# Start places of a matmul's two SBUF operands modulo 256 bytes, in a float32r block on one core

## What is computed

```python
proj   = rms_norm(h) @ w_in                        # 272 rows, 7176 columns
h      = h + merged @ w_out
q      = rms_norm(h) @ w_query
a      = gelu(u @ hb)   # PEER: all 16384 experts  (peer_u)
h      = h + (g * a) @ v                           # (peer_v)
proj_2 = rms_norm(h) @ w_in_2                      # 256 rows from here on
h      = h + (attn @ w_attn_br * gate1 + ssm @ w_ssm_br * gate2) @ w_out_2
h      = h + (silu(conv(x @ w_up)) * ...) @ w_down
```

## The kernel before

| tile | start | start modulo 256 | step from one feature tile to the next |
|---|---|---|---|
| `hhi`, `hlo` [128, 16, 272] | 16,512 and 33,920 | 128 | 1088 bytes = 4 x 256 + 64 |
| `whi`, `wlo` | 67,712 and 75,904 | 128 | 512 bytes from one 128 x 128 block to the next |
| `fox_hi`, `ask_hi`, `ysh`, `mhi` and their low parts [.., 256] | in `big` (84,096) | 128 | 1024 bytes |
| `early` [128, 2, 16, 272] | in `big` | 128 | 1088 bytes |

## Time and profile before

### The profile page before, as it was taken

One profiled execution on the slowest core, in us unless ns is written; L12 is line 12 of the kernel. 1 busy time (PEld: TensorE's weight loads), 2 busy tenths in 40 slices (PEclk: granted clock), 3 DMA queues, 4 the chain that ended last, 5 costly groups with the idle time before them and its releaser, 6 DMA issues.

```text
span 3572.0 us, 75102 instructions
## 1 busy us (share of the span) xinstructions
PE 3530.3 (99%) x26786; PEld 3340.6 (94%) x26786; DVE 2650.0 (74%) x4903; ACT 2076.8 (58%) x3860; POOL 104.1 (3%) x169
## 2 busy tenths in 40 slices
PE   7999999999999999999999999999999999999999
PEld 6999999999999999787788889999999999999999
DVE  7875687688888888555688877998657686666555
ACT  5455655677767777455455556664565565555554
POOL 1000020000000000000000000000000000000000
PEclk9999999999999999999999999999999999999999
DMA  8854487455555555565788874554455555556555
GB/s 308 328 192 144 148 295 277 149 187 183 186 177 165 165 164 162 163 215 187 265 329 329 329 246 139 171 160 155 145 180 185 183 184 183 187 183 186 185 185 173
DMA packets 184770, 721.33 MB, mean 202 GB/s; under 512 B 20512, under 2 KB 23072, under 8 KB 171808
## 3 DMA queue, kind: packets, MB, share of 16 engines
q1 hardware_dynamic: 167328, 608.57, 52.5%
q0 software_dynamic: 14496, 103.82, 8.2%
q10 hardware_dynamic: 2784, 6.78, 0.5%
HBM read 714.89 MB, written 4.19 MB: 201 GB/s over the span
## 4 chain that ended last, share of the span: by engine, by line
PE 96%; DVE 3%; ACT 1%; DMA 1%; issue 0%; SPq 0%; DVEq 0%; ACTq 0%
PE PS L444 24%; PE PS L446 23%; PE PS L445 23%; PE PS L583 7%; PE PS L584 6%; PE PS L585 6%; PE PS L804 1%; PE PS L850 0%; PE PS L669 0%; DMA raw<-peer_v_dram 0%; DVE big L1562 0%; PE PS L596 0%; DVE wlo L1492 0%; PE PS L779 0%; PE PS L617 0%
## 5 line engine op out<-in xcount | busy, mean ns | idle before, releaser
L444 PE MATMUL PS<-hhi,whi 128*128 128x256 f32 (+1 forms) x6208 | 1758.9, 283 | 13.2 <-DVE hlo L1553 10.5
L445 PE MATMUL PS<-hlo,whi 128*128 128x256 f32 (+1 forms) x6208 | 1751.2, 282 | 0.0
L446 PE MATMUL PS<-hhi,wlo 128*128 128x256 f32 (+1 forms) x6208 | 1750.4, 282 | 0.0
L989 ACT ACTIVATE whi<-raw 128x512 fp32r<-128x512 f32 x1832 | 1139.8, 629 | 1045.3 <-PE PS L446 690.7
L1492 DVE TENSOR_TENSOR wlo<-raw,whi 128x512 fp32r<-128x512 f32 x1448 | 976.2, 690 | 578.5 <-ACT whi L989 573.8
L444 PEld LDWEIGHTS PS<-hhi,whi 128*128 128x128 f32 x6208 | 1174.0, 189 | 25.6 <-issue 22.2
L446 PEld LDWEIGHTS PS<-hhi,wlo 128*128 128x128 f32 x6208 | 1175.0, 189 | 0.0
L445 PEld LDWEIGHTS PS<-hlo,whi 128*128 128x128 f32 x6208 | 1167.9, 188 | 0.6
L1623 DVE TENSOR_TENSOR wlo<-raw,whi 128x512 fp32r<-128x512 f32 x596 | 409.0, 700 | 167.4 <-ACT whi L1077 113.7
L1077 ACT ACTIVATE whi<-raw 128x512 fp32r<-128x512 f32 x468 | 292.6, 630 | 292.3 <-PE PS L446 290.5
L583 PE MATMUL PS<-whi,hhi 128*128 128x512 f32 x1024 | 403.9, 394 | 3.9 <-issue 2.2
(11 more groups left out here) (463 smaller groups left out, 3391.9 us busy)
## 6 DMA issues: line engine op xcount, KB each, us to landing
raw<-peer_u_dram SPq DMA_DIRECT2D x256, 512.0 KB, 3.5
raw<-peer_v_dram SPq DMA_DIRECT2D x256, 512.0 KB, 4.2
raw<-w_in_dram SPq DMA_DIRECT2D x240, 512.0 KB, 3.6
big<-w_mod_dram POOLq DMA_DIRECT2D x96, 1024.0 KB, 5.3
raw<-w_up_dram SPq DMA_DIRECT2D x176, 512.0 KB, 3.5
raw<-w_down_dram SPq DMA_DIRECT2D x88, 512.0 KB, 3.5
raw<-w_out_dram SPq DMA_DIRECT2D x64, 512.0 KB, 3.6
raw<-w_query_dram SPq DMA_DIRECT2D x32, 512.0 KB, 4.5
```

Source lines behind the costliest of these rows:

```text
L444: pe.matmul(out, hi, rhi, start=start, stop=False, **more)
L445: pe.matmul(out, hi, rlo, start=False, stop=False, **more)
L446: return pe.matmul(out, lo, rhi, start=False, stop=stop, **more)
L989: f(whi[:, m % PAIRS, quarter(q)], raw[:, m % RING, quarter(q)], ACT.Copy).then_inc(hi_ready, 1)
```

## The change

Three things, with no instruction added, removed or moved on any engine:

1. Two more names, `thi` and `tlo`, lie over the same bytes as `hhi` and `hlo` (16,512 and 33,920), with rows of 256 elements: [128, 16, 256], a step of 1024 bytes. Everything behind `w_in` reads and writes them in place of `hhi[.., META:]`. `w_in` keeps `hhi`, `hlo` and their step. `early` gets a step of 320 elements (1280 bytes = 5 x 256).
2. `mod` (384 bytes) is allocated ahead of `whi`, so that `whi` and `wlo` start at 68,096 and 76,288: 0 modulo 256.
3. `rstd` (2176 bytes) is allocated behind `wlo`, so that `big` moves by 2560 bytes in all and keeps its place, 128 modulo 256. `rstd` itself goes from 128 to 0 modulo 256, and with it `rows_bf` and one of the four `cols_three`, which lie over it.

Behind `w_in` every input tile now starts at 128 modulo 256 and every block of weights at 0: the distance is 128 for all of them. In `w_in` the four distances come as 128, 192, 0, 64 (narrow: 192, 0, 64, 128), the same ring entered at another place.

```diff
         hhi = nc.alloc_sbuf_tensor_at("hhi", [P, KC, KEYS], F32R, offset=at)
         hlo = nc.alloc_sbuf_tensor_at("hlo", [P, KC, KEYS], F32R, offset=at + KC * KEYS * 4)
+        thi = nc.alloc_sbuf_tensor_at("thi", [P, KC, SEQ], F32R, offset=at)
+        tlo = nc.alloc_sbuf_tensor_at("tlo", [P, KC, SEQ], F32R, offset=at + KC * KEYS * 4)
         raw = sb("raw", [P, RING, HALF])
+        mod = sb("mod", [P, N_MOD * KC])
         whi = sb("whi", [P, PAIRS, HALF], F32R)
         wlo = sb("wlo", [P, PAIRS, HALF], F32R)
+        at_rstd = -(-nc.sbuf_base // 32) * 32
+        rstd = sb("rstd", [P, 2, KEYS])
         at_big = -(-nc.sbuf_base // 32) * 32
         big = sb("big", [P, 128 * SEQ])
...
         vecs = sb("vecs", [P, 240])
-        mod = sb("mod", [P, N_MOD * KC])
         gmod = sb("gmod", [P, KC])
-        at_rstd = -(-nc.sbuf_base // 32) * 32
-        rstd = sb("rstd", [P, 2, KEYS])
...
-        early = nc.alloc_sbuf_tensor_at("early", [P, 2, KC, KEYS], F32R, offset=at_big + 4 * 24 * SEQ)
+        early = nc.alloc_sbuf_tensor_at("early", [P, 2, KC, 320], F32R, offset=at_big + 4 * 24 * SEQ)
...
-                                hi, lo = (hhi[:, half * 8:, o:], hlo[:, half * 8:, o:]) if halves is None else halves[half]
+                                hi, lo = (thi[:, half * 8:, :], tlo[:, half * 8:, :]) if halves is None else halves[half]
...
-                o = KEYS - width
+                hi, lo = (t[:, :, KEYS - width:] for t in (hhi, hlo)) if name == "w_in" else (thi, tlo)
...
-                                             wlo[:, half, at_], hhi[:, b % 2, META:], hlo[:, b % 2, META:],
+                                             wlo[:, half, at_], thi[:, b % 2, :], tlo[:, b % 2, :],
...
-                                    o_ = slice(META + t * P, META + (t + 1) * P)
+                                    o_ = slice(t * P, (t + 1) * P)
...
-                    f(hhi[:, base + k * group:base + (k + 1) * group, o:], src[:, k * group:(k + 1) * group, :],
+                    f((hhi if o == 0 else thi)[:, base + k * group:base + (k + 1) * group, :], src[:, k * group:(k + 1) * group, :],
```

More of the change, by code:

```diff
@@ L580, in body @@
                                 for t in range(2):
-                                    o_ = slice(META + t * P, META + (t + 1) * P)
+                                    o_ = slice(t * P, (t + 1) * P)
                                     bank = PS[:, t * 4 + half * 2 + q, :]
-                                    pe.matmul(bank, hhi[:, b % 2, o_], whi[:, half, quarter(q)], start=opens, stop=False, skip_group_check=True)
-                                    pe.matmul(bank, hhi[:, b % 2, o_], wlo[:, half, quarter(q)], start=False, stop=False, skip_group_check=True)
-                                    last = pe.matmul(bank, hlo[:, b % 2, o_], whi[:, half, quarter(q)], start=False,
+                                    pe.matmul(bank, thi[:, b % 2, o_], whi[:, half, quarter(q)], start=opens, stop=False, skip_group_check=True)
+                                    pe.matmul(bank, thi[:, b % 2, o_], wlo[:, half, quarter(q)], start=False, stop=False, skip_group_check=True)
+                                    last = pe.matmul(bank, tlo[:, b % 2, o_], whi[:, half, quarter(q)], start=False,
                                                      stop=False, skip_group_check=True)
@@ L750, in _ @@
                 for half in range(2):
-                    hi, lo = (fox_hi, fox_lo) if half == 0 else (hhi[:, 0:8, META:], hlo[:, 0:8, META:])
+                    hi, lo = (fox_hi, fox_lo) if half == 0 else (thi[:, 0:8, :], tlo[:, 0:8, :])
                     for kc in range(8):
@@ L949, in _ @@
                 dense_turn("w_out_2", 320, SEQ, g, None, SPLITS["ys"] if g == 0 else None,
-                           ((hhi[:, 8:, META:], hlo[:, 8:, META:]), (mhi, mlo)), shift=2)
+                           ((thi[:, 8:, :], tlo[:, 8:, :]), (mhi, mlo)), shift=2)
             def early_chunk(g, c):
@@ L1454, in up_turn @@
                         sc.wait_ge(quarters_used, 2 * (PAIRS + FIRST["w_down"] - 2) + 1)
-                        f(hhi[:, 0, META:], act[:, 0, :], ACT.Copy).then_inc(stage_hi, 1)
+                        f(thi[:, 0, :], act[:, 0, :], ACT.Copy).then_inc(stage_hi, 1)
                     split(g, FIRST["w_up"], 2 * k + 2)
@@ L1504, in split_input @@
                     where = slice(base + k * group, base + (k + 1) * group)
-                    dv.tensor_tensor(hlo[:, where, o:], src[:, k * group:(k + 1) * group, :], hhi[:, where, o:],
+                    dv.tensor_tensor(tlo[:, where, :], src[:, k * group:(k + 1) * group, :], thi[:, where, :],
                                      ALU.subtract).then_inc(in_ready, 1)
@@ L1778, in low_tiles @@
                 tiles = slice(4 * k, 4 * k + 4)
[L1779 removed]
+                dv.tensor_tensor(tlo[:, tiles, :], hm[:, tiles, :], thi[:, tiles, :], ALU.subtract).then_inc(in_ready, 1)
             def plain_tiles(k):
@@ L2207, in merged_low @@
             def merged_low(q):
-                hi, lo = (t[:, 8 + 4 * q:12 + 4 * q, META:] if q < 2 else m[:, 4 * q - 8:4 * q - 4, :]
-                          for t, m in ((hhi, mhi), (hlo, mlo)))
+                hi, lo = (t[:, 8 + 4 * q:12 + 4 * q, :] if q < 2 else m[:, 4 * q - 8:4 * q - 4, :]
+                          for t, m in ((thi, mhi), (tlo, mlo)))
                 dv.wait_ge(in_hi, SPLITS["ys"] + q + 1)
```

37 lines of the change are left out of this document (18 added, 19 removed).

## The result

The changed kernel takes **3590.48 us** (median of 12 runs, 3583.34 to 3594.41) against 3577.82 (12 runs, 3573.46 to 3583.23): ratio 1.0032, 95% interval 1.0024 to 1.0040, some 9 to 14 us slower. The forecast was 3579.0, with a range up to 3588. The profiled execution has a span of 3581.3 us and is the quickest of the twelve, as that of before (3572.0) was near its own lower end.

A forecast was written before the change was run, and what follows sets the result against it. TensorE was taken as the bound: number of matmuls times the distance between their starts. The terms summed to +1.1 us, 3572.0 to 3573.1 profiled, and with the median's 5.9 us to 3579.0 us, range 3562 to 3588.

The forecast's parts named there:

- Term 5: `early`, 258 columns, from four distances in turn to 128 alone: 119.9 to 119.5 ns, -0.4 us.
- Term 1: Dense stages on `hhi`, from four distances in turn to 128 alone: 13,824 matmuls from 118.3 to 118.6 ns, +3.7 us.
- the step from span to median: Whole kernel: the runs' median stands 5.9 us above the profiled span, and the same was added to the forecast.
- Rivals A: All dense matmuls: distance 128 is a fast pairing at 117.8 ns or lower, -13.8 us, 3564 us; chance 0.24.
- B: Every matmul behind `w_in`: input's own place at 128 costs, 120.0 ns throughout, +28.5 us, 3606 us; chance 0.12.
- Rival C: All stages: the distance isn't taken modulo 256, gains and losses mix, within 7 us of 3578; chance 0.07.
- Term 2: Stages on `ask_hi`, `fox_hi`, `mhi`, `ysh`, from distance 0 to 128: 1,728 matmuls from 120.0 to 118.6 ns, -2.4 us.
- Terms 3: `w_down`, even blocks from distance 64 to 128: 1,056 matmuls, +0.8 ns each, +0.8 us; odd blocks 0.
- 4: `peer_v`, 512 columns, even tiles from 192 to 128: 1,536 matmuls, -0.4 ns each, -0.6 us.
- 6: `w_in`: the four distances are entered two steps later in the same order, 0.
- 7: ScalarE and VectorE splits change place but hide behind TensorE: bounded by +1 and -1 us, taken as 0.
- 8: Some 700 short matmuls beside `peer_u`, on `rstd` and `rows_bf`: between -1.5 and +1.5 us, taken as 0.

The follow-up runs named there:

- before_third: The kernel before, unchanged, profiled a third time: span 3578.2 us.
- after_third: The changed kernel, unchanged, profiled a third time: span 3589.5 us.
- early256: The changed kernel with the two additional columns of the early `w_up` matmuls left out (256 columns, rows still 1280 bytes): 3582.18 us, one execution.
- early272: The changed kernel with the rows of `early` back at 272 elements: 3583.09 us (12 runs), ratio to the kernel before 1.0015.
- d64: The changed kernel with weights at 64 modulo 256, input still at 128 (distance 64): 3567.47 us (6 runs), ratio to the kernel before 0.9968.
- d192: The changed kernel with weights at 192 modulo 256 (distance 192): 3509.83 us in one execution; timed again 3521.22 us (5 runs), ratio to the kernel before 0.9823.
- d0: The changed kernel with weights at 128 modulo 256, same as the input (distance 0): 3588.59 us (7 runs), ratio to the kernel before 1.0028.

## Why the prediction was wrong

The forecast was +1.1 us. The step that failed is in the sum: terms 5 and 1, both priced from neighbouring rows as if a distance had one price for every width and stage. By the traces the distances cost +7.4 us. That alone would put the median near 3585, inside the range; another 5 us, which the forecast put at nothing when it took the step from span to median for a constant, took it out. Their cause stays in part open.

**Right: what bounds, and the distance as the one quantity.** The counts are the same, TensorE's pace is what moved, and 118.7 ns settled in `w_query`, `w_glu`, `peer_u`, `w_out_2`, `w_up`, the branches and `w_down`. Rivals A and B are out: 128 is not the fast pairing, and with the input at 128 any price from 113.3 to 120.0 is to be had. Rival C is out too: 192 bytes ahead and 64 bytes back give the same.

**Term 1 was too small: +3.7 forecast, some +5.8 measured.** The odd blocks of `w_down` do average 118.6 in the trace of before, but settled, with every block at 128, the price is 118.67. 118.33 and 118.67 are 0.34 apart, not 0.27: on `peer_u` (775.9 to 777.9 us), the later `w_up` (363.4 to 364.4) and the branches that is 3.3 us. `w_in_2` went from 428.8 to 430.7 us between `before_third` and `after_third`, 1.9 where 0.34 ns would give 1.0: with attention products in between, its matmuls average 118.8 (118.15 before), since some 200 to 290 of them run at 120.0. And `w_out` runs at 120.0 ns altogether, some 0.5 us more on its half on `thi`. "The forecast, a settled 118.6 ns" took one distance to have one price.

**Term 2: -2.4 forecast, -1.7 measured.** `w_query` -1.0, `w_glu` -0.2, `mhi` -0.45; the half on `fox_hi` stayed at 120.0.

**Terms 3, 4, 6, 7, 8.** `w_down` +1.0 (forecast +0.8). `peer_v` between -0.8 and 0 (forecast -0.6): its pattern wanders within 232.1 to 233.3. `w_in` keeps its distances. VectorE's split takes 691 ns and ScalarE's 630, where they took 690 and 629, and TensorE's waits for `wlo` did not grow (some 4 us in both profiles). The 720 short matmuls on `rows_bf` (term 8) start 56.8 ns apart in both kernels: 0, as taken.

**Term 5 failed: -0.4 forecast, +2.7 measured.** "A column costs 0.44 ns" was taken from whole steps of 256 columns. 258 columns at a fixed 128 settle elsewhere. This is the largest single miss, and `early256` shows it to be the two columns, `early272` that the old ring avoids it. Why two columns do this no run shows.

Together the distances give 5.8 - 1.7 + 1.0 - 0.4 + 2.7 = +7.4 us, in line with the 6 us left above without the clock.

**The step from the profile to the median was wrong as well.** I took the 5.9 us between span and median for a constant. About 2 us of it are outside the span (3583.34 against 3581.3 in the changed kernel's profiled run); the rest was that this execution of the kernel before had little low clock, and executions of one kernel scatter by some 10 us. The changed kernel's median lies 12.7 us above, 5 more than the distances explain. In the profiles it has 8 us more of half clock on average (32 against 24), worth up to 4. The mean granted clocks of the timed executions say the same, more weakly: 0.994 over the twelve of the changed kernel, 0.995 over 38 of the kernel before. At one clock, 0.995, they average 3587.5 us (4) and 3578.0 (14), 9.5 apart, so the clock is not all of it. The same few us stand between the changed kernel's median and other versions: `d64` is 23 us below it where its distances give 16, `early272` 7.4 where they give 2.7. Whether the change brings this about, by pausing at other moments, or whether these twelve executions were dear ones, stays open: the scatter within one kernel is as large.

A sentence on the notes: the Trainium skill ("TensorE: Matmul & The Clock Gate", "Step-by-step: what each phase is for") has two independent read ports for the moving stream and the weight loads, so that loading the next weights takes no read bandwidth from the running matmul. The runs here don't fit that: only start places were changed, and the same 2400 matmuls took from 272.0 us (`d192`) to 288.0 (`d0`). By what mechanism the two reads meet, no run shows.

## What to carry to other kernels

Where TensorE alternates a weight load with a float32r matmul of some 256 columns and is the bound, as here, look at where the two operands lie against each other in SBUF; sweep the distance in steps of 64 bytes in the kernel itself and read the pace of each stage from the timeline, because shapes differ (0 is worst for 256 columns and best for 512 here) and a price at one distance can't be interpolated from its neighbours. Time several executions, since one distance can have two paces. Here 192 gave 1.8%, while the 128 of the change cost 0.3%. Make rows whole multiples of 256 bytes only with the distance chosen, and don't carry a per-column price over to a width that is two columns past one that was measured.

## What was not expected of the hardware

- The pace of back-to-back 256-column matmuls goes from 113.3 to 120.0 ns by the distance alone. At 192 it has two stable patterns, 113.3 and 117.8 ns. Without a hole in the stream it keeps the one it entered for thousands of matmuls; at a hole, 0.01 us more or less went with the one or the other, and one program scatters from 3505.79 to 3527.75 us. The 113.3 turns up for short stretches at distance 64 as well.
- 512-column matmuls take 226.7 ns at distance 0, 228.9 at 64 and 232 to 233.3 at all other distances tried.
- Two columns beyond 256 cost 0.9 ns at distance 0, 3.5 at 128 and 4.4 at 64.
- With distance and shape fixed, what is left of the scatter between executions of one kernel (3572.0 to 3578.2 us, 3581.3 to 3589.5) goes with how long the clock stood at half after TensorE's waits and small products: 17, 24 and 31 us in the order of the spans before, 24, 27, 34 and 41 us for spans of 3581.3, 3582.6, 3584.4 and 3589.5 us.
